# A hybrid decoder block on one Trainium2 core: the feed-forward's second product as seven block products in four chunks

## The reference, cut to what matters

```python
D_MODEL, SEQ, D_FF = 1024, 512, 4096
x = x + rms_norm(merged @ w_o, norm_mix_post)
hf = rms_norm(x, norm_ff_pre)
ff = jnp.square(jax.nn.relu(hf @ w_ff_in)) @ w_ff_out      # (512x1024 @ 1024x4096), (512x4096 @ 4096x1024)
return x + rms_norm(ff, norm_ff_post)
```

## Time and profile before

| | |
|---|---|
| median of 3 runs | 802.95 us (802.93 to 804.87) |
| profiled execution, its own time | 805.02 us |
| its span in the trace | 803.3 us |
| PE busy | 790.7 us, 98% of the span |
| DVE busy | 415.5 us, 52% |
| ACT busy | 322.2 us, 40% |
| POOL busy | 60.4 us, 8% |
| mean granted TensorE clock | 0.994 of full speed |
| DMA | 80.22 MB, 100 GB/s on average |

### The profile page before, as it was taken

One profiled execution on the slowest core, in us unless ns is written; L12 is line 12 of the kernel. 1 busy time (PEld: TensorE's weight loads), 2 busy tenths in 40 slices (PEclk: granted clock), 3 DMA queues, 4 the chain that ended last, 5 costly groups with the idle time before them and its releaser, 6 DMA issues.

```text
span 803.3 us, 10375 instructions
## 1 busy us (share of the span) xinstructions
PE 790.7 (98%) x3736; PEld 660.4 (82%) x3736; DVE 415.5 (52%) x730; ACT 322.2 (40%) x561; POOL 60.4 (8%) x110
## 2 busy tenths in 40 slices
PE   7999999999999999999999999999999999999996
PEld 6888888888887888888888988888888888888885
DVE  5624667777777238866536654442323354432334
ACT  4522656656565742232344444322112344322211
POOL 2000000122232003000002300000000000000001
PEclk8999999999999999999999999999999999999999
DMA  8243222212222631345231343322323333322202
GB/s 288 87 124 104 77 82 78 80 53 85 74 79 59 204 99 59 105 149 184 87 104 47 87 134 126 104 100 84 105 82 103 94 89 104 104 82 103 78 1 104
DMA packets 96214, 80.22 MB, mean 100 GB/s; under 512 B 3120, under 2 KB 77872, under 8 KB 96176
## 3 DMA queue, kind: packets, MB, share of 16 engines
q1 hardware_dynamic: 95504, 79.70, 31.6%
q10 hardware_dynamic: 672, 0.01, 0.0%
HBM read 77.60 MB, written 2.10 MB: 99 GB/s over the span
## 4 chain that ended last, share of the span: by engine, by line
PE 96%; DVE 2%; DMA 1%; ACT 1%; issue 0%; SPq 0%; DVEq 0%; POOLq 0%; POOL 0%; ACTq 0%
PE acc L1126 30%; PE acc L1127 30%; PE acc L1128 30%; PE aux L1313 1%; DMA g_pre<-in_norm_mix_pre 1%; PE aux L1239 1%; PE aux L1238 1%; PE aux L1248 1%; PE acc L1267 1%; PE acc L1264 1%; PE aux L1221 1%; PE aux L1168 1%; DVE x L819 0%; DVE actB_lo L810 0%; ACT probs L673 0%; DVE scores_sb L939 0%
## 5 line engine op out<-in xcount | busy, mean ns | idle before, releaser
L800 DVE TENSOR_TENSOR w_lo<-w_raw,w_hi 128x1024 fp32r<-128x1024 f32 x132 | 161.4, 1224 | 199.9 <-ACT w_hi L564 199.3
L564 ACT ACTIVATE w_hi<-w_raw 128x1024 fp32r<-128x1024 f32 x132 | 138.9, 1054 | 192.4 <-PE acc L1128 190.2
L1126 PE MATMUL acc<-actB_hi,w_hi 128*128 128x512 f32 (+1 forms) x544 | 207.0, 381 | 0.0
L1128 PE MATMUL acc<-actB_hi,w_lo 128*128 128x512 f32 (+1 forms) x544 | 205.2, 377 | 0.0
L1127 PE MATMUL acc<-actB_lo,w_hi 128*128 128x512 f32 (+1 forms) x544 | 205.0, 377 | 0.0
L1128 PEld LDWEIGHTS acc<-actB_hi,w_lo 128*128 128x128 f32 x544 | 102.4, 188 | 19.1
L1127 PEld LDWEIGHTS acc<-actB_lo,w_hi 128*128 128x128 f32 x544 | 102.5, 188 | 18.2
L1126 PEld LDWEIGHTS acc<-actB_hi,w_hi 128*128 128x128 f32 x544 | 102.4, 188 | 18.1
L1126 PE MATMUL acc<-w_hi,ff_hi 128*128 128x512 f32 x256 | 101.0, 395 | 0.0
L1128 PE MATMUL acc<-w_hi,ff_lo 128*128 128x512 f32 x256 | 101.0, 395 | 0.0
L1127 PE MATMUL acc<-w_lo,ff_hi 128*128 128x512 f32 x256 | 101.0, 394 | 0.0
(11 more groups left out here) (163 smaller groups left out, 895.9 us busy)
## 6 DMA issues: line engine op xcount, KB each, us to landing
w_raw<-in_w_in SPq DMA_DIRECT2D x44, 512.0 KB, 3.8
w_raw<-in_w_ff_in SPq DMA_DIRECT2D x32, 512.0 KB, 4.0
w_raw<-in_w_ff_out SPq DMA_DIRECT2D x32, 512.0 KB, 3.7
w_raw<-in_w_b SPq DMA_DIRECT2D x8, 512.0 KB, 3.5
w_raw<-in_w_a SPq DMA_DIRECT2D x8, 512.0 KB, 3.5
w_raw<-in_w_o SPq DMA_DIRECT2D x8, 512.0 KB, 3.7
x<-in_x SPq DMA_DIRECT2D x4, 512.0 KB, 7.5
x<-in_x SPq DMA_DIRECT2D x1, 2048.0 KB, 8.3
```

The source lines that it names most:

```text
L564: nc.scalar.activation(w_hi[:, j], w_raw[:, j], ACT.Copy).then_inc(hi_made, 1)
L800: nc.vector.tensor_tensor(w_lo[:, j], w_raw[:, j], w_hi[:, j].bitcast(F32), ALU.subtract).then_inc(lo_made, 1)
L1126: nc.tensor.matmul(o, a_hi, b_hi, start=first, stop=False)
L1128: return nc.tensor.matmul(o, a_lo, b_hi, start=False, stop=last)
```

## The change

The second product of the feed-forward is computed by Strassen's scheme (in the form with 15 additions). The activations of a chunk, as a matrix of tokens x inner columns, are cut into 2x2 blocks, the weights too (output columns in two halves, inner rows by odd and even units of 128), and seven block products take the place of eight. The inner columns go in four chunks (`CHUNKS`), each with 8 column units, then seven products of two weight units each (`PRODUCTS`, in the order P1, P5, P6, P7, P4, P3, P2). A unit of a product is 2 x 2 x 3 = 12 matmuls of 512 columns: two inner blocks, two token tiles p of one token half or of a sum of both.

- **Left sums.** For each pair of column units DVE makes four sums of 128x256 (`s_raw`), and hi and lo are made of seven blocks (`op_hi`, `op_lo`) in place of four.
- **Right sums.** GpSimd makes eight differences of 128x1024 floats per chunk (`weight_sum`, `SUMS`), in the order T1a, T1b, T3a, T2a, T2b, T3b, T4a, T4b; a and b are the two units of a product. P5 uses T1, P6 T2, P7 T3, P4 T4. T1, T2 and T4 share one buffer, so T2 waits for the lo part of P5, and T4 for that of P6.
- **Loads.** `w_ff_out` comes as four loads of 1 MB per chunk into `down_raw`, between the loads of `w_ff_in`. After the first six these alternate between two slots of `w_raw`.
- **Banks.** P1, P6, P4 and P2 take turns in banks 0 and 1 of `acc` (`ROTATING`), and are added to `sum1`, `sum6`, `sum4`, `sum2` after each chunk's product (by ACT in chunk 0, by DVE after). P5, P7 and P3 stay in PSUM through all chunks. From chunk 1 on the column units use banks 0 and 1 too.
- **The end.** In the last chunk DVE merges the products into the four quarters of the output, applies the gain and adds the residual. Stores are one each for token tiles 2 and 3, and two each for tiles 0 and 1.

```diff
+CHUNKS = 4
+FF_UNITS = FF // P // CHUNKS
+PAIRS = FF_UNITS // 2
+PRODUCTS = ["P1", "P5", "P6", "P7", "P4", "P3", "P2"]
+ITEMS = FF_UNITS + 2 * len(PRODUCTS)
+LEFT = {"P1": 0, "P2": 1, "P4": 2, "P5": 3, "P6": 4, "P7": 5, "P3": 6}
+ROTATING = ["P1", "P6", "P4", "P2"]
+SUMS = ["T1a", "T1b", "T3a", "T2a", "T2b", "T3b", "T4a", "T4b"]
...
 @block.sync
+            def load_up(m):
+                if m < SLOTS:
+                    slot_free(U_FF + m)
+                else:
+                    before = m - 4 if m < 6 else m - 2
+                    sp.wait_ge(lo_made, U_FF + ff_unit(before) + 1)
+                load_columns(m if m < SLOTS else m % 2, w_ff_in_v, slice(m * P, (m + 1) * P))
...
+            for c in range(1, CHUNKS):
+                for n in range(FF_UNITS):
+                    load_up(c * FF_UNITS + n)
+                    if 2 <= n < 2 + PAIRS:
+                        load_down(c, n - 2)
...
 @block.gpsimd
+                if name[:2] == "T2":
+                    pool.wait_ge(lo_made, U_FF + product_item(c, "P5", h) + 1)
+                if name[:2] == "T4":
+                    pool.wait_ge(lo_made, U_FF + product_item(c, "P6", h) + 1)
+                nc.gpsimd.tensor_tensor(o, x, y, ALU.subtract).then_inc(t_made, 1)
...
 @block.scalar
+                r = product_item(c, name, h)
+                act.wait_ge(pe_done, UNIT_DONE[U_FF + r - SLOTS])
+                nc.scalar.activation(moving(w_hi, r % SLOTS), right_raw(name, h), ACT.Copy).then_inc(hi_made, 1)
...
+                        nc.scalar.activation(op_hi[:, j, 1:3].rearrange("p a s -> p (a s)"), ff_act[:, m % 4],
+                                             ACT.Copy).then_inc(op_hi_made, 1)
+                        act.wait_ge(s_made, 4 * (c * PAIRS + j + 1))
+                        nc.scalar.activation(op_hi[:, j, 3:7].rearrange("p a s -> p (a s)"),
+                                             s_raw[:].rearrange("p a s -> p (a s)"),
+                                             ACT.Copy).then_inc(op_hi_made, 1)
+                for name in PRODUCTS:
+                    for h in range(2):
+                        hi_ahead(product_item(c, name, h))
+                    if c == 0 and name in ROTATING:
+                        dst = {"P1": sum1, "P6": sum6, "P4": sum4, "P2": sum2}[name]
+                        for p in range(2):
+                            act.wait_ge(pe_done, BANK_DONE[U_FF + product_item(c, name, 1), p])
+                            nc.scalar.activation(dst[:, p], acc[:, p], ACT.Copy).then_inc(taken, 1)
...
 @block.vector
+                        nc.vector.tensor_tensor(s_raw[:, 0], e[:, 2 * P:S], f[:, 2 * P:S],
+                                                ALU.add).then_inc(s_made, 1)
+                        dve.wait_ge(s_made, count + 2)
+                        nc.vector.tensor_tensor(s_raw[:, 1], s_raw[:, 0], e[:, 0:2 * P],
+                                                ALU.subtract).then_inc(s_made, 1)
+                        dve.wait_ge(s_made, count + 3)
+                        nc.vector.tensor_tensor(s_raw[:, 3], f[:, 0:2 * P], s_raw[:, 1],
+                                                ALU.subtract).then_inc(s_made, 1)
...
+                for name in PRODUCTS:
+                    for h in range(2):
+                        at = FF_UNITS + 2 * PRODUCTS.index(name) + h
+                        lo_ahead(item(c, at))
+                    if 0 < c and not last and name in ROTATING:
+                        dst = {"P1": sum1, "P6": sum6, "P4": sum4, "P2": sum2}[name]
+                        for p in range(2):
+                            bank_done(name, p)
+                            nc.vector.tensor_tensor(dst[:, p], acc[:, p], dst[:, p], ALU.add).then_inc(taken, 1)
...
 @block.tensor
+            def operands(c, name, h):
+                pe.wait_ge(lo_made, U_FF + product_item(c, name, h) + 1)
+                pe.wait_ge(op_lo_made, 3 * (c * PAIRS + 2 * h + 1) + {"P1": 1, "P4": 2, "P2": 2}.get(name, 3))
...
+                    if c == 0:
+                        pe.wait_ge(relu_made, n - 3)
+                    elif n < 2:
+                        pe.wait_ge(taken, 8 * c - 1 + n)
+                    else:
+                        pe.wait_ge(relu_made, c * FF_UNITS + n - 1)
+                    m = columns_unit(item(c, n) % SLOTS, actB, n % (4 if c == 0 else 2))
```

More of the change, by code:

```diff
@@ L125, in _pe_counts @@
     rows(U_WO + SLOTS, SLOTS, inside=0)
[L126 to L130, removed]
+    for c in range(CHUNKS):
+        columns(U_FF + item(c, 0), FF_UNITS)
+        for name in PRODUCTS:
+            u = U_FF + product_item(c, name, 0)
+            if (c, name) != (CHUNKS - 1, PRODUCTS[-1]):
+                n += 1
+                unit_done[u] = n
+            for p in range(2):
+                n += 1
+                bank_done[u + 1, p] = n
+            unit_done[u + 1] = n
     return unit_done, bank_done
@@ L445, in _ @@
                     load_rows(j, w_o_v, 2 * j, bass.ds(b * COL, COL))
[L446 to L459, removed]
@@ new lines, in load_down @@
+            def load_down(c, j):
+                if c:
+                    sp.wait_ge(lo_made, U_FF + item(c, 0))
+                elif j >= 2:
+                    sp.wait_ge(turned, T_FF + TT)
+                k = c * FF_UNITS + 2 * j
+                sp.dma_start(down_raw[:, j], w_ff_out_v[:, k:k + 2, :]).then_inc(down_loaded[j], 16)
+            for m in range(SLOTS):
+                load_up(m)
+            load_up(4)
+            load_up(5)
+            sp.wait_ge(a_lo, GROUPS)
+            load_down(0, 0)
@@ L468, in _ @@
+            for n, t in enumerate((2, 3)):
+                sp.wait_ge(y_made, n + 1)
+                sp.dma_start(out_v[:, t], x1[:, t]).then_inc(stored, 16)
+            for n, (t, h) in enumerate(((0, 1), (0, 0), (1, 1), (1, 0))):
+                cols = slice(h * COL, (h + 1) * COL)
+                sp.wait_ge(y_made, 2 + n + 1)
+                sp.dma_start(out_v[:, t, cols], x1[:, t, cols]).then_inc(stored, 16)
+            sp.wait_ge(stored, 16 * 6)
         @block.gpsimd
@@ L787, in _ @@
+            for p in range(2):
+                ff_square(4 + p, sum1[:, p], 1, p)
+            for p in range(2):
+                ff_square(6 + p, sum2[:, p], 0, p)
         @block.vector
@@ new lines, in item_product @@
+            def item_product(c, name, h, p):
+                r = product_item(c, name, h)
+                resident = name not in ROTATING
+                for jj in range(2):
+                    j = 2 * h + jj
+                    at = (slice(None), j, LEFT[name], slice(p * P, (p + 1) * P))
+                    hi, lo = moving(w_hi, r % SLOTS)[:, jj], moving(w_lo, r % SLOTS)[:, jj]
+                    m = product(BANKS[name][:, p], (op_hi[at], op_lo[at]), (hi, lo),
+                                j == 0 and (not resident or c == 0),
+                                j == PAIRS - 1 and (not resident or c == CHUNKS - 1))
+                return m
```

396 lines of the change are left out of this document (264 added, 132 removed).

## The result

The changed kernel takes **827.21 us** (median of 4 runs, 825.71 to 829.3) against 802.98 us before: 1.0298 times as long, 95% interval 1.0267 to 1.0329. It is slower by 24.2 us. Slower was the likeliest outcome of the prediction, but by 4.9 us, and 827 lies outside its range of 795 to 814.

A forecast was written before the change was run, and what follows sets the result against it. TensorE, busy for 98% of the span, was taken to bound the kernel. -22.3 + 10.9 + 11.2 + 5.1 = +4.9 us, put on the median, gave 807.9 us, with a range of 795 to 814.

The forecast's parts named there:

- What is removed: Second feed-forward product: 672 matmuls instead of 768, at 0.232 us each, 22.3 us less.
- Chunk to chunk: Three chunk ends: TensorE waits for bank 0's free, behind weight parts and unit 3's late load; 10.9 us more.
- I take 0.9: Chunk ends: unit 3's load lands 0.9 us after P2's end, chosen from 0.8 to 2.3.
- my slow end: Chunk ends: unit 3's load lands 2.3 us after P2's end, 8.3 us after the first issue.
- The left sums: P5's second unit, four chunks: GpSimd's T2b and T3b block VectorE's short sums, delaying op_lo; 11.2 us more.
- one of the sums that I had cost at nothing: Column stage: T1a, T1b, T3a and T2a meet VectorE there, covered by 11 us per pair of units; 0 us.
- The end: After TensorE's last matmul: VectorE's merges, gains and residual adds end the span 11.5 us later, before 6.4; 5.1 us more.
- The clock: Rival: clock falls behind 4.1 us waits after chunks 1 and 2, 2 to 4 us more; 0.17 together with column-stage starvation.
- The range: Whole kernel: 795 to 814 us, leaving out 2 in 10.
- the load term: Unit 3's load within the chunk-end sum of 10.9 us: 8.2 if loads are in time, 15.1 at the slowest.

The follow-up runs named there:

- run 10: Change with bank frees first, T2b/T3b later, reordered end and last frees moved; additionally each GpSimd weight sum covers only 64 of 1024 columns: 783.42 us.
- run 1: Against the change: in every product the instructions freeing its bank stand between the two hi or lo parts of its turn, not behind both: 804.55 us.
- run 2: Against the change: each GpSimd weight sum replaced by three memsets of the same tile, which read nothing from SBUF: 810.01 us.
- run 5: Against the change: from T2b on, GpSimd's weight sums of a chunk wait until all op_lo of the chunk are made: 828.09 us.
- Run 3: Against the change: from chunk 1 on the four 1 MB loads of w_ff_out go out behind column units 4 to 7, not 2 to 5: 819.99 us.
- run 4: Against the change: TensorE multiplies zeros during the waits at chunk ends (8 matmuls after chunk 0, 16 after chunks 1 and 2): 820.19 us.
- run 7: Change with bank frees first and T2b/T3b later, plus residual adds of token tiles 2 and 3 moved behind the last two banks' gains: 797.99 us.

## Why the prediction was wrong, step by step

- **What is removed.** 22.3 us predicted, 23.0 found (run 10 against before). Right.
- **Chunk to chunk.** 10.9 predicted, 19.4 found. The mechanism was right to the instruction, as run 1 shows by taking it away. The term mis-sized is "I take 0.9" for the late load of unit 3. I had chosen near the fast end on the thought that the first loads are partly done. In the trace it was 2.3 after chunk 0, which is my slow end, and 4.3 and 4.4 after chunks 1 and 2, which is 2 us beyond it: 2 MB issued from 619.9 on had landed at 630.1, 10.2 us, where my own slow end from the earlier trace rows said 8.3 after the first issue. From 2 to 6 us behind the first issue, at the end of chunk 0 and then of chunk 1 (the last two numbers are DMA share and GB/s):

```profile
528.50:530.50 2.00, 2.00 (x10) 1.67 (x9) 0.73 (x1) 0.04 (x1) 0.00 (x0) 1.00 1.12 368
530.50:532.50 2.00, 1.86 (x9) 1.17 (x7) 0.95 (x1) 1.02 (x1) 0.00 (x0) 1.00 1.00 401
...
621.90:623.90 2.00, 2.00 (x10) 1.67 (x9) 0.72 (x1) 0.00 (x0) 0.00 (x0) 1.00 1.16 244
623.90:625.90 2.00, 1.85 (x8) 1.16 (x7) 0.85 (x1) 1.06 (x1) 0.00 (x0) 1.00 0.57 219
```

The same loads in the same order moved fewer bytes in the second case. With this order unit 3's load took 5.4 to 5.8 us at most chunk ends and 7.5 to 9.2 at the others (chunks 1 and 2 in the change and in run 2, chunk 2 in runs 1, 5 and 10); why is open. Run 3 confirms that the 1 MB loads make it late, though not whether the one ahead or the one right behind, since both moved: without them the load takes 3.9 to 4.1 us, and these waits fall by 8.4 us in sum.

- **The left sums.** 11.2 predicted, 13.3 found: 2.6 in chunks 1 to 3 where I had 2.8, and 5.5 in chunk 0. A weight sum took 2.4 to 2.6 us alone, 3.3 when it waits for VectorE. Run 2 shows the reads to be the cause. What I missed is chunk 0: VectorE comes out of its first four units late, and T2a, one of the sums that I had cost at nothing, then holds up `op_lo` of 128x256 in front of P1 (2.6 us for a 0.42 us operation).
- **The end.** 5.1 predicted, 3.9 found (10.2 us instead of 6.4, where I had 11.5).
- **The clock.** Here the forecast failed most. It stood among the rivals, at 2 to 4 us, and was not in the sum. It cost 11.0 us, nearly all in matmuls at half clock. I had it only behind the two longest waits; the trace has it behind five: the three at the chunk ends, that of 3.9 us at P5 in chunk 0, and one of the three of 2.6 us at P5, in chunk 1. Three of these places cost 7.1 us, and run 4 shows that the idle time is the cause there.
- **The range.** 814 was the forecast with one rival added. A late load and a slow clock are not alternatives: the load makes the wait longer and the longer wait lowers the clock. With the slow end of the load term (15.1 in place of 10.9, so 9.1 in place of 4.9) and the 11.0 us of clock that the trace has, the same working gives 803.0 + 9.1 + 11.0 = 823.1 us. That is an argument from hindsight; what the runs show is that both terms exist and add.
- **Open.** Of three waits of 2.6 us at P5 the change has half clock behind that of chunk 1 alone, run 1 behind that of chunk 3 alone, and run 3 behind all three (2.6 and 2.7 us there); why was not tried. Run 3's clock loss (12.3 us, more than the change's 11.0, with shorter waits) is part of the same question. Open is also why unit 3's load lands 2 us later at some chunk ends than at others.

## What to carry to other kernels

Where an engine executes in order, look at what stands ahead of the instruction that frees a buffer: here a free behind two weight preparations turned a late load, harmless by itself, into a stall of TensorE at every chunk, and moving it took 22.7 us off. A fraction of an algorithm saved (an eighth of the matmuls, 23 us) is an upper bound; price each wait that it adds with the clock that the wait costs, and add mechanisms that feed each other instead of setting them side by side. Sums on GpSimd that read SBUF are not free beside VectorE operations with two SBUF inputs, whichever of the two has nothing to do on the average.

## What the hardware showed that I had not expected

- A wait of TensorE of 2.4 us at P5 (2.6 by the ledger's measure) was followed by 5 distances of 0.43 us in chunk 1 and by none in chunks 2 and 3, where the waits were the same; I had thought of waits of over 3 us.
- The slowdown between GpSimd and VectorE is mutual and stacks: a sum of 2.5 us alone took 3.3 us behind a VectorE operation, and a `w_lo` of 1.23 us took up to 3.4 us between two sums.
- Filling an idle gap of VectorE with a two-input operation lengthened the chain that it was to hide in, by 0.9 us (run 7).
